# The two sums of the turned S5 input moved from VectorE to GpSimd, and the scan one step later

## What is computed

```
# S5 (layer 1): complex-diagonal recurrence over time, s_t = a * s_(t-1) + B u_t
xr = einsum('bsgc,gpc->bsgp', u, bbr);  xi = einsum('bsgc,gpc->bsgp', u, bbi)
_, _, sr, si = associative_scan(combine, (a_r, a_i, xr, xi), axis=1)
y = einsum('bsgp,gcp->bsgc', sr, c_re) - einsum('bsgp,gcp->bsgc', si, c_im)
y = y + d_skip * hf;  g = gelu(y);  out = g * sigmoid(g @ glu_w + glu_b)

# PEER (both layers): idx and gate come from the top-k
act = gelu(einsum('td,tkd->tk', xb, u_tab[idx]))
y   = einsum('tk,tkd->td', gate * act, v_tab[idx])
```

## Time and profile before

| | us |
|---|---|
| time, median of 3 runs | 1553.74 |
| lowest and highest of the 3 | 1551.52, 1554.93 |
| the profiled execution | 1553.37 |
| its span in the trace | 1551.6 |

### The profile page before, as it was taken

How to read it: one execution, slowest core, us unless ns; L and a number is a source line. 1 busy time by engine, 2 the same in 40 slices (tenths; PEclk the granted TensorE clock), 3 DMA queues, 4 the chain that set the end, 5 groups by cost and what they waited for, 6 DMA issues and landing times.

```text
span 1551.6 us, 19133 instructions
## 1 busy us (share of the span) xinstructions
PE 1097.8 (71%) x5920; PEld 348.4 (22%) x5920; DVE 1111.5 (72%) x2533; ACT 770.2 (50%) x2120; POOL 589.4 (38%) x517
## 2 busy tenths in 40 slices
PE   7997678866765666679866575656878666666665
PEld 3542222322211212223221121212323111111110
DVE  2356887479787899985477799999456866666554
ACT  2315554445456667764334666766334644444433
POOL 0024343323443354554334345344432443434430
PEclk9998689878966776879988567686998777676675
DMA  9569999999999998999999999999999999999995
GB/s 358 179 234 413 420 405 418 414 415 408 415 421 421 354 374 358 410 421 415 412 413 414 403 357 369 355 363 406 380 416 415 415 422 421 421 421 421 421 422 234
DMA packets 105418, 603.39 MB, mean 389 GB/s; under 512 B 9314, under 2 KB 9442, under 8 KB 39780
## 3 DMA queue, kind: packets, MB, share of 16 engines
q0 software_dynamic: 73728, 536.90, 84.8%
q1 hardware_dynamic: 31588, 65.26, 11.3%
HBM read 601.08 MB, written 1.05 MB: 388 GB/s over the span
## 4 chain that ended last, share of the span: by engine, by line
DMA 32%; DVE 31%; PE 22%; ACT 7%; issue 3%; DVEq 3%; ACTq 1%; POOL 1%; SPq 0%; POOLq 0%
DMA rings<-in_uv_tab_dram,idx 24%; DVE rings L1324 11%; PE ps L715 9%; PE ps L920 8%; DMA wst<-in_wq_dram 7%; DVE mem L1231 2%; PE ps L908 2%; DVE dgs L1324 2%; ACT dgs L667 1%; DVE mem L1213 1%; ACT wgt L664 1%; DMA rings<-in_w_in_dram 1%; DVE mem L1242 1%; ACT L661 1%; DVE mem L1240 1%
## 5 line engine op out<-in xcount | busy, mean ns | idle before, releaser
L920 PE MATMUL ps<-rings,dgs 64*64 64x512 f32 x3648 | 638.0, 804 | 343.3 <-ACT dgs L667 342.6
L463 POOL DMA_INDIRECT rings<-in_uv_tab_dram,idx x456 | 521.7, 1144 | 804.3 <-PE ps L920 687.8
L1324 DVE CUSTOM_DVE_ANT_0 rings<-rings,h 128x1024 f32<-128x1024 f32 x456 | 550.7, 1224 | 210.8 <-DMA rings<-in_uv_tab_dram,idx 197.7
L661 ACT ACTIVATE gel<-dots 128x1 f32<-128x1 f32 x512 | 102.1, 199 | 522.2 <-DVE dots L1324 518.5
L920 PEld LDWEIGHTS ps<-rings,dgs 64*64 64x64 f32 x3648 | 128.3, 163 | 783.4 <-ACT dgs L667 682.3
L667 ACT ACTIVATE dgs<-cst,wgt 128x128 f32<-128x128 f32 x512 | 205.6, 402 | 36.3 <-issue 1.5
L715 PE MATMUL ps<-wst,hT 128*128 128x512 f32 x320 | 168.0, 666 | 37.1 <-DMA wst<-in_wq_dram 20.5
L664 ACT ACTIVATE wgt<-gel,share 128x1 f32<-128x1 f32 x512 | 150.8, 295 | 35.5 <-issue 0.3
L920 PE MATMUL ps<-dgs 64*64 64x512 f32 x448 | 80.2, 795 | 53.2 <-ACT dgs L667 53.1
L463 POOL DMA_INDIRECT dgs<-in_uv_tab_dram,idx x56 | 65.9, 1176 | 88.3 <-PE ps L920 74.8
L715 PEld LDWEIGHTS ps<-wst,hT 128*128 128x128 f32 x320 | 63.4, 212 | 138.1 <-issue 134.9
(11 more groups left out here) (192 smaller groups left out, 991.2 us busy)
## 6 DMA issues: line engine op xcount, KB each, us to landing
wst<-in_wq_dram SPq DMA_DIRECT2D x15, 2048.0 KB, 28.2
wst<-in_w_out_dram SPq DMA_DIRECT2D x4, 2048.0 KB, 22.8
wst<-in_glu_w_dram SPq DMA_DIRECT2D x4, 2048.0 KB, 31.7
rings<-in_uv_tab_dram,idx POOLq DMA_INDIRECT x456, 15.7
rings<-in_w_in_dram SPq DMA_DIRECT2D x3, 2048.0 KB, 16.7
rings<-in_w_in_dram SPq DMA_DIRECT2D x2, 1024.0 KB, 7.5
dgs<-in_w_in_dram SPq DMA_DIRECT2D x1, 2048.0 KB, 19.4
vec<-in_vecs_dram SPq DMA_DIRECT2D x3, 512.0 KB, 17.2
```

Source lines behind the costliest of these rows:

```text
L463: nc.gpsimd.indirect_dma_start(out=ring[g % RING], out_offset=None, in_=uv_tab, in_offset=bass.IndirectOffsetOnAxis(ap=idx[n % AHEAD][:, s ...
L661: A.activation(gel[i][:, every], dots[i][:, every], ACT.Gelu_apprx_tanh)
L920: ins = PE.matmul(ps[64 * b:64 * b + 64, 4 + 2 * t + half, :], diag[rows, g % DIAGS, rows], ring[g % RING][rows, D + b * BANK:D + (b + 1) ...
L1324: V.tensor_tensor_reduce(out=u, in0=u, in1=h[:, t, :], scale=1.0, scalar=0.0, op0=ALU.mult, op1=ALU.add, accum_out=dots[n % 2][:, s:s + 1] ...
```

## The change

Two edits. (1) DVE's `s5_add` goes. GpSimd gets a stage of that name with the same two sums: it waits until the turning is done (`w_ok`), does the real and the imaginary sum, and raises a new semaphore `add_ok`. GpSimd walks the same table of stages, but POOL_LAG = 6 steps behind its own gathers: the sums of block c of tile 0 stand between the gathers of steps 146 + 9c and 147 + 9c. (2) DVE's scan moves one step later, ahead of step 143 + 9c (from `slot + 3` to `slot + 4`), and starts with a wait for `add_ok`; the small addition of tile 1 now stands in front of it. The turning back stays where it was.

```diff
--- before.py
+++ after.py
@@ -35,6 +35,7 @@
 EXPERTS = NK * NK
 GROUPS = 2 * T * PH
 RING = 9
+POOL_LAG = 6
 AHEAD = 16
 PACE = 1
 DIAGS = 16
@@ -168,7 +169,7 @@
             at(g, slot, ("s5_decay", t, c))
             at(g, slot + 1, ("s5_rot", t, c))
             at(g, slot + 2, ("s5_add", t, c))
-            at(g, slot + 3, ("s5_scan", t, c))
+            at(g, slot + 4, ("s5_scan", t, c))
             at(g, slot + 4, ("s5_cmat", t, c))
             at(g, slot + 5, ("s5_back", t, c))
             if c + 1 < KC:
@@ -320,6 +321,7 @@
         got = [sem(f"got{b}") for b in range(RING)]
 
         r_ok, rd_ok, sn_done, dt5_ok, dd_ok = (sem(n) for n in ("r_ok", "rd_ok", "sn_done", "dt5_ok", "dd_ok"))
+        add_ok = sem("add_ok")
         sq_done, ms_done, sd_done, h_done, nT_done, hT_act, hT_dve, x_done, w_used = (sem(n) for n in (
             "sq_done", "ms_done", "sd_done", "h_done", "nT_done", "hT_act", "hT_dve", "x_done", "w_used"))
 
@@ -452,8 +454,24 @@
             nc.gpsimd.affine_select(out=sg3, in_=sg3, pattern=[[0, 8], [1, P]], compare_op=ALU.is_ge, fill=0.0, base=0,
                                     channel_multiplier=-1).then_inc(sgm_ok, 1)
 
+            def s5_add(t, c):
+
+                pool.wait_ge(w_ok, KC * t + c + 1)
+                nc.gpsimd.tensor_tensor(by_cos[:, 0, :, :], by_cos[:, 0, :, :], by_sin[:, 1, :, :], ALU.add)
+                nc.gpsimd.tensor_tensor(by_cos[:, 1, :, :], by_cos[:, 1, :, :], by_sin[:, 0, :, :],
+                                        ALU.subtract).then_inc(add_ok, 1)
+
+            stage = dict(s5_add=s5_add)
+
+            def run(stages):
+                for name, *args in stages:
+                    if name in stage:
+                        stage[name](*args)
+
             for g in range(GROUPS * TOPK):
                 n, s = g // TOPK, g % TOPK
+                if g >= POOL_LAG:
+                    run(WORK[(g - POOL_LAG) // TOPK].get((g - POOL_LAG) % TOPK, []))
                 if s == 0:
                     pool.wait_ge(idx_ok, n + 1)
                 if g < RING and g % 2 == 0:
@@ -1214,17 +1232,13 @@
                 V.tensor_tensor(by_sin, x4, sin, ALU.mult).then_inc(w_ok, 1)
                 dve.drain()
 
-            def s5_add(t, c):
-                V.tensor_tensor(by_cos[:, 0, :, :], by_cos[:, 0, :, :], by_sin[:, 1, :, :], ALU.add)
-                V.tensor_tensor(by_cos[:, 1, :, :], by_cos[:, 1, :, :], by_sin[:, 0, :, :], ALU.subtract)
-                dve.drain()
+            def s5_scan(t, c):
+
+                dve.wait_ge(add_ok, KC * t + c + 1)
                 if t == 1:
 
                     V.tensor_tensor(by_cos[:, :, :, 0], by_cos[:, :, :, 0], z_last[:, :, 4 * c:4 * c + 4], ALU.add)
                     dve.drain()
-
-            def s5_scan(t, c):
-
                 dve.wait_ge(dt5_ok, KC * t + c + 1)
                 for r in range(2):
                     w = by_cos[:, r, :, :].rearrange("p j s -> p (j s)")
@@ -1328,7 +1342,7 @@
                          att_max=att_max, att_den=att_den, sgu_var=sgu_var, sgu_norm=sgu_norm, sgu_gate=sgu_gate, mix=mix,
                          mixT_copy=mixT_copy, w_sum=w_sum, q_copy=q_copy, y_sum=y_sum, s5_n=s5_n, s5_k=s5_k,
                          s5_b0=s5_b0, s5_b1=s5_b1, s5_rot=s5_rot,
-                         s5_frac=s5_frac, s5_add=s5_add, s5_scan=s5_scan, s5_back=s5_back, glu_sum=glu_sum, norm_r=norm_r)
+                         s5_frac=s5_frac, s5_scan=s5_scan, s5_back=s5_back, glu_sum=glu_sum, norm_r=norm_r)
             stage |= dict(route_keys=route_keys, route_pairs=route_pairs, route_best=route_best, route_index=route_index,
                           route_gate=route_gate)
```

## The result

The changed kernel takes 1568.77 us (median of 4 runs, 1568.42 to 1569.49), the kernel before, run beside it, 1554.34: the ratio is 1.0097, with a 95% interval of 1.0085 to 1.0109, or 13 to 17 us more. The forecast was 1561.2 with 1544 to 1571. The time lies inside that range, the direction held and so did most of the mechanism, but the size did not: +14.4 us instead of +7.8. The profiled execution took 1568.42, its span is 1566.7, and its counterpart of before 1551.6.

What follows compares the result with a forecast made beforehand. VectorE was taken to bound 12 of 16 blocks, DMA covering tile 0's blocks 4 to 7. Blocking of 24.7 us less 16.9 saved gives +7.8 on 1553.4: 1561.2 us, range 1544 to 1571.

Steps and rivals of the forecast that it cites:

- The bounds at the twelve blocks: Tile 0 blocks 0 to 3 and tile 1's 8 blocks: VectorE bounds, so work removed or added counts in full.
- Rival 1: GpSimd's sums and VectorE run side by side without blocking; faster, 1545.5 us, or 1540.5 with 0.8 us sums; chance 0.20.
- rival 2: Balance: GpSimd's sums and VectorE exclude each other, but a sum takes near 0.8 us; 1552.7 us; chance 0.16.
- The scan's move: VectorE's scan one step later: costs no time by itself, the same instructions standing in another order.
- Rival 3: Sums delay gathers past their 6 us lead, VectorE waits for them in S5 stretches; 1570; chance 0.14 with long sums.
- What is saved: The two sums and drain leave VectorE: 1.41 us a block at 12 blocks, 16.9 us at most.
- about half of the blocks: Expected in the changed profile: VectorE waits for `add_ok` at about half of the blocks, 2 us each.
- early: 5 blocks where GpSimd's gather is issued before the turning ends: dot products wait for the sums, 2.0 us each.
- late: 6 blocks where TensorE, and so GpSimd's gather, is behind: VectorE waits for `add_ok`, 2.3 us each.
- covered: Tile 1 block 3: first sum lies beside VectorE's one-operand routing, the second sticks out by 0.9 us.
- in both directions: Tile 0's blocks 4 to 7: DMA covers VectorE work taken off or laid on, so they count as nothing.
- I cost it at nothing: Gathers queued behind the sums on GpSimd are held some 3 us; their lead absorbs it, cost nothing.

Runs made afterwards that it cites:

- experiment 3: Kernel before, sums kept on VectorE, plus two unused sums on constants on GpSimd at the change's place, nobody waiting: 1586.08 us, ratio 1.021.
- experiment 7: Kernel before plus two unused GpSimd sums, begun once the dot product ahead of the turning is done, beside VectorE's PSUM multiplications: 1567.28 us, ratio 1.0094.
- experiment 1: Kernel before with only the scan moved one step later, sums staying on VectorE: 1552.94 us, ratio 0.9994.
- experiment 12: The change at tile 0 blocks 0 to 3 and all of tile 1 only, the other four blocks as before: 1565.36 us, ratio 1.0071.
- experiment 6: The change at blocks 4 to 7 of tile 0 alone, the others as in the kernel before: 1556.10 us, ratio 1.002.
- 2, no sums: Kernel before with the two sums left out on every engine, all else in place: 1538.64 us, ratio 0.9898.
- Experiment 4: Kernel before plus three unused GpSimd fills of a spare buffer per block, which write and read nothing: 1558.23 us, ratio 1.0032.
- experiment 11: Changed kernel with scan and fraction a further step later, at slot + 5: 1567.19 us, ratio to the kernel before 1.0085.
- experiment 10: Kernel before with the sums done by TensorE matmuls into PSUM, scan and fraction both at slot + 5: 1546.92 us, ratio 0.9964.

## Why the prediction was right and wrong

**Right.**

- *The bounds at the twelve blocks.* There 25.5 us of excess laid on VectorE put the stream back by 25.3 (experiment 3, table below).
- *The sums and VectorE exclude each other while VectorE reads two on-chip operands*, and not while it reads PSUM (experiments 3 and 7). Rival 1 is out. So is rival 2: a sum takes 1.27 us, not 0.8. My 1.2, midway between the bounds, was short by 0.07. The estimate from the Trainium skill (GPSIMD Engine Reference, Elementwise: side-by-side cycle accounting), 1.12, was short by 0.15.
- *The scan's move is free* (experiment 1).
- *The gathers' delay is free at the twelve blocks at lag 6.* VectorE waits for no gather in the two stretches, and what the stream falls behind is what is laid on VectorE. At blocks 4 to 7 of tile 0 this isn't shown (point 3). Rival 3, gathers running dry within the S5 stretches, didn't come. Where GpSimd waits long for VectorE ahead of its gathers there are signs of it, at the end: 1.26 us at step 339 in experiment 7.
- *What is saved.* 16.9 us forecast, 14.9 (13 to 19) measured.

The forecast wait for `add_ok` at "about half of the blocks" came true in number, 8 of 16, but partly by luck: four of the eight are at blocks that the prediction had put at nothing.

**Wrong**, by its own steps. The blocked time of the changed kernel, each instruction's excess and each wait for `add_ok` read block by block:

| kind of block | forecast | measured in the trace |
|---|---|---|
| early, 5 | 5 x 2.0 = 10.0 | 2.02, 1.87, 1.86, 2.69, 1.83 = 10.3 |
| late, 6 | 6 x 2.3 = 13.8 | 2.39, 2.46, 2.23, 2.38, 3.46, 2.87 = 15.8 |
| covered, 1 | 0.9 | 2.95 |
| sum | 24.7 | 29.1 |
| saved | -16.9 | -16.9 (1.41 x 12) |
| net at the 12 blocks | +7.8 | +12.2, as a whole kernel +11.0 (experiment 12) |
| tile 0, blocks 4 to 7 | 0 | +2.5 (experiment 6) |
| the change | +7.8 | +13.5 to +14.7; measured +14.4 |

1. The step *Covered* failed. It said that the routing "reads one operand" and that one sum lies beside it. Its top-8 searches aren't held up beside a sum (experiment 3); but the addition of 974.73 stood still for both sums. About 2 us here: 2.95 instead of 0.9. (Redone from rows 11 and 12, with the sums begun 0.3 us behind 964.01, the step gives 0.6, so the miss is a little larger.) Such an instruction took the first of the two blocks at three of the five early blocks and the second at a fourth, where a dot product would have otherwise, so nothing was lost there.
2. The step *Late* was 2.0 us short, for two reasons. At block 3 of tile 0 and block 6 of tile 1 the instruction ahead of the sums stood still for both sums instead of taking turns, 2.5 and 2.9 us. And at block 4 of tile 1 GpSimd was later than I had read, so that the wait was 3.5. VectorE there:

```profile
1004.05 0.08 DVE L1338 DVE_READ_ACCUMULATOR2_ANT dots<- 128x1 f32 x1
1007.60 0.17 DVE L1240 TENSOR_TENSOR mem<-mem,z_last 128x8 f32<-128x8 f32 x1 [3.46 <-POOL mem L461]
```

and GpSimd:

```profile
1004.09 0.94 POOL L481 DMA_INDIRECT rings<-in_uv_tab_dram,idx  x1 [0.30 <-PE ps L938]
1005.06 1.29 POOL L460 TENSOR_TENSOR mem<-mem 128x512 f32<-128x512 f32 x1
1006.29 1.27 POOL L461 TENSOR_TENSOR mem<-mem 128x512 f32<-128x512 f32 x1
```

VectorE is through with its dot products at 1004.13. GpSimd has still to issue a gather, of 1004.09, which TensorE releases that late. In the forecast the same wait began when the gather was already through, and so had to be the sums' 2.4 us at most.

3. The step *in both directions* failed: "tile 0's blocks 4 to 7 are covered by DMA". It holds for a gain and not for a loss. VectorE was through well ahead of GpSimd at these blocks and waited 2.4, 3.4, 2.4 and 3.4 us in the changed kernel, and the change at these blocks alone cost 2.5 us (experiment 6), where the forecast has 0.

The traces show where each run loses, by the start of the dot product of a given step. For example step 175 starts at 615.99 us before and 618.66 in experiment 7, and step 212 like this, before and then in experiment 7:

```profile
703.39 1.23 DVE L1324 CUSTOM_DVE_ANT_0 rings<-rings,h 128x1024 f32<-128x1024 f32 x1 [1.25 <-DMA rings<-in_uv_tab_dram,idx]
710.27 1.22 DVE L1338 CUSTOM_DVE_ANT_0 rings<-rings,h 128x1024 f32<-128x1024 f32 x1 [1.25 <-DMA rings<-in_uv_tab_dram,idx]
```

So experiment 7 falls back by 6.9 - 2.7 = 4.2 us between the two. The table has this for three stretches, in us, and in brackets what was laid on VectorE there (excess and waits for the sums) less the 1.41 a block taken off. Each is one execution; experiment 1, where all should be near 0, has 0.1, 0.9 and -0.4.

| run | tile 0, blocks 0 to 3 (steps 139 to 175) | tile 0, blocks 4 to 7 (175 to 212) | tile 1 (267 to 339) |
|---|---|---|---|
| the change | 3.5 (3.1) | 3.1 (5.9) | 8.8 (9.0) |
| 2, no sums | -5.7 (-5.6) | 0.8 (-5.6) | -10.0 (-11.3) |
| 3, spare sums | 8.1 (8.1) | 4.6 (8.3) | 17.2 (17.4) |
| 4, only writes | 0.7 (1.3) | 2.2 (0.4) | 1.2 (1.6) |
| 6, blocks 4 to 7 | 0.0 (0) | 3.5 (4.9) | -0.1 (0) |
| 7, beside the turning | 0.2 (0) | 4.2 (0) | 4.1 (2.2) |
| 11, later scan | 2.1 (1.8) | 4.1 (0.7) | 5.7 (6.0) |
| 12, the other twelve | 3.7 (3.4) | 0.5 (0) | 8.4 (8.5) |

For the change and experiments 3, 11 and 12 the first and the last column follow the brackets to 0.4 us: this is what "VectorE bounds" means. The middle column doesn't follow them. Taking work off VectorE gained nothing there, and experiment 7 lost 4.2 us with nothing laid on VectorE. By step 212 VectorE waits 1.0 to 1.3 us for its gather in every run of the table, so what is lost up to there is what the gathers lost. They lose when GpSimd is held, by a wait or by its own sums, as well as when VectorE is late. So besides the cover, the step *I cost it at nothing*, the gathers' delay, is in doubt at these four blocks. Experiment 4 holds up the gathers there and lays hardly anything on VectorE, and loses 2.2 us, against 3.1 in the changed kernel and 3.5 in experiment 6. With a scatter of about 1 us the held gathers may thus be most of it. How the loss of these blocks divides between them and VectorE's waits stays open.

The sum of the table is made from one execution and agrees with the measurement to 1 us; how the last microsecond divides between points 1 to 3 is not settled. Why a VectorE instruction sometimes gets in between the sums and sometimes not isn't either. At the four places of the changed kernel where it stood still for both (block 3 of tile 0, blocks 3, 5 and 6 of tile 1), it had begun 0.1 to 0.6 us ahead of the first sum, during a gather's issue or its end; where it began at or behind the start of a sum, it waited for that one alone. In experiment 11 one dot product that began 0.2 us behind it stood still for both all the same.

## What to carry to other kernels

Work that leaves a bounding VectorE for GpSimd pays only if it runs while VectorE reads PSUM or waits: beside instructions with two on-chip operands it blocks them, here 2.1 us laid on for 1.41 taken off. Small copies and TENSOR_SCALAR instructions are no cover, top-8 searches are. Then ask what GpSimd itself holds up by waiting for that moment, here the gathers: that was free where VectorE bounded and cost time where DMA did. And "covered by DMA" is a statement about work taken off VectorE; a loss has to be priced by itself. Of the three ways to do the sums off VectorE, only TensorE's won, and it did only when the instruction that is moved was looked at as cover for what stands behind it (28.3 us of waits at one place, none at the other).

## What the runs showed of the hardware that I had not expected

- A GpSimd sum of 128x512 fp32 with two operands: 1.26 to 1.28 us undisturbed, up to 2.32 behind a dot product of VectorE.
- A VectorE dot product that is begun during a gather's issue can stand still for two GpSimd instructions in a row: 3.91 and 4.09 us instead of 1.22.
- One-operand TENSOR_SCALAR instructions of 128x16 numbers on VectorE (0.16 to 0.23 us) stand still beside GpSimd's sums, up to 3.11 us, and beside GpSimd's fills that only write, up to 0.95 us. A dot product beside such a fill keeps its 1.22, and MAX8, FIND_INDEX8 and MATCH_REPLACE8 keep their length beside both (28 beside sums, 12 beside fills, 0.01 us more at most).
- Extra matmuls on TensorE went with faster ones of the others: with 16 more instructions a block the granted clock is 0.83 instead of 0.71 from 880 to 1085 us (experiment 10), and one of the experts' takes 764 ns instead of 884.
